# Two-block transformer kernel on one core: the RWKV triangular solve for both token tiles in common steps, gate scaling on GpSimd, constant tables in three transfers

## What is computed

```python
proj = (h @ w_in[l]).astype(jnp.float32)
ret_c, fox_c, rwkv_c, gate_c = jnp.split(proj, splits, axis=-1)
y_ret = _retention_branch(ret_c, ...)
y_fox = _fox_branch(fox_c, ...)
y_rwkv = _rwkv7_branch(rwkv_c, ...)
gates = jax.nn.sigmoid(gate_c)            # three gates of width 1024
merged = gates0 * (y_ret @ p_ret) + gates1 * (y_fox @ p_fox) + gates2 * (y_rwkv @ p_rwkv)
x = x + merged @ w_out[l]
x = x + (silu(g) * u) @ w_down[l]         # g, u = split(rmsnorm(x) @ w_gate_up[l])
```

## Time and profile before

| | us |
|---|---|
| median of 3 runs | 1142.59 (1142.31 to 1143.15) |
| the profiled execution | 1143.25 |
| its span | 1141.5 |
| PE busy | 1119.3 (98%) |
| DVE busy | 791.3 (69%) |
| ACT busy | 551.9 (48%) |
| POOL busy | 55.0 (5%) |
| chain that ended last, PE's share | 79% |

### The profile page before, as it was taken

The page is one execution under the profiler, slowest core; times in us unless marked ns, Lnnn a source line. Parts: engine busy times, 40 slices in busy tenths (PEclk is TensorE's granted clock), DMA queues, the critical chain, the costliest instruction groups (busy, mean ns, idle before and its releaser), DMA issues.

```text
span 1141.5 us, 22331 instructions
## 1 busy us (share of the span) xinstructions
PE 1119.3 (98%) x9556; PEld 1017.8 (89%) x9556; DVE 791.3 (69%) x1135; ACT 551.9 (48%) x768; POOL 55.0 (5%) x43
## 2 busy tenths in 40 slices
PE   9799999999999999999999999999999999999997
PEld 7689999899999998889998899999998778987687
DVE  6597765877555566887665966555567677877885
ACT  6355443534333344465443544333336675756762
POOL 0012000200000000102001000000000010001000
PEclk9899999999999999999999999999999999999998
DMA  9543334536453435542335356345344435363320
GB/s 365 212 173 113 112 113 153 205 125 240 202 219 137 196 140 217 175 158 98 126 113 205 128 207 236 144 189 220 147 148 171 167 114 197 133 227 111 113 110 38
DMA packets 27762, 188.28 MB, mean 165 GB/s; under 512 B 3488, under 2 KB 4384, under 8 KB 6048
## 3 DMA queue, kind: packets, MB, share of 16 engines
q1 hardware_dynamic: 26096, 175.89, 41.2%
q10 hardware_dynamic: 1440, 8.55, 1.9%
q0 software_dynamic: 144, 2.66, 0.5%
HBM read 181.84 MB, written 5.24 MB: 164 GB/s over the span
## 4 chain that ended last, share of the span: by engine, by line
PE 79%; DVE 9%; ACT 4%; DMA 2%; issue 1%; DVEq 1%; POOL 1%; POOLq 0%; ACTq 0%
PE bank L1149 21%; PE bank L696 14%; PE bank L1165 11%; PE bank L752 10%; PE bank L1129 4%; PE bank L1111 4%; DVE in_low L1971 2%; PE bank L1298 2%; PE bank L845 2%; ACT scratch L1526 2%; PE bank L861 1%; DMA table<-tables_dram 1%; PE bank L884 1%; ACT in_high L1459 1%; PE bank L684 1%
## 5 line engine op out<-in xcount | busy, mean ns | idle before, releaser
L696 PE MATMUL bank<-in_low,h_high 128*128 128x512 f32 x336 | 131.9, 393 | 0.0
L1149 PE MATMUL bank<-h_high,gate_split 128*128 128x256 f32 x704 | 128.8, 281 | 0.2
L1149 PE MATMUL bank<-h_high,up_split 128*128 128x256 f32 x704 | 128.6, 280 | 0.0
L1165 PE MATMUL bank<-act_split,down_split 128*128 128x256 f32 x960 | 118.5, 283 | 0.0
L696 PE MATMUL bank<-in_high,h_high 128*128 128x512 f32 x272 | 110.1, 405 | 6.7 <-DVE in_low L1971 6.0
L1165 PEld LDWEIGHTS bank<-act_split,down_split 128*128 128x128 f32 x960 | 116.6, 192 | 0.0
L752 PE MATMUL bank<-h_high,in_high 128*128 128x256 f32 x384 | 115.8, 301 | 0.5 <-DVE in_low L1971 0.5
L1149 PEld LDWEIGHTS bank<-h_high,gate_split 128*128 128x128 f32 x704 | 109.9, 189 | 0.8 <-DVE h_low L1913 0.6
L1459 ACT ACTIVATE in_high<-ring 128x2048 fp32r<-128x2048 f32 x46 | 87.7, 1910 | 47.0 <-PE bank L696 35.9
L1149 PEld LDWEIGHTS bank<-h_high,up_split 128*128 128x128 f32 x704 | 109.8, 189 | 0.0
L752 PE MATMUL bank<-x_low,in_high 128*128 128x256 f32 x384 | 108.4, 282 | 0.0
(11 more groups left out here) (380 smaller groups left out, 2509.3 us busy)
## 6 DMA issues: line engine op xcount, KB each, us to landing
ring<-w_in_dram SPq DMA_DIRECT2D x70, 1024.0 KB, 4.9
ring<-w_gate_up_dram SPq DMA_DIRECT2D x44, 1024.0 KB, 8.3
ring<-w_down_dram SPq DMA_DIRECT2D x22, 1024.0 KB, 4.9
ring<-w_out_dram SPq DMA_DIRECT2D x16, 1024.0 KB, 6.5
ring<-p_all_dram SPq DMA_DIRECT2D x6, 1024.0 KB, 4.8
x_kept<-scratch ACTq DMA_DIRECT2D x4, 1024.0 KB, 3.9
x<-x_kept ACTq DMA_DIRECT2D x4, 1024.0 KB, 7.6
table<-tables_dram POOLq DMA_DIRECT2D x1, 2594.0 KB, 13.7
```

The source lines that it names most:

```text
L696: last = mm(bank[(n - n % 2 + t) % 4][:], a, b, start=c == 0 and i == 0, stop=c == KT - 1 and i == 2)
L1149: last = mm(bank[2 * half + part][:, f * S:(f + 1) * S], a, b, start=k == 0 and i == 0, stop=k == KT - 1 and i == 2)
L1165: last = mm(bank[4 + m // 2][:, m % 2 * S:(m % 2 + 1) * S], a, b, start=first and m % 2 == 0 and k == 0 and i == 0, stop=end and m % 2 == ...
```

## The change

It does three things. (1) The solve runs both token tiles in the same steps: a level's product on PE holds both tiles, with two pieces of fill after it, and DVE's mask and addition are twice as wide. The buffers that both tiles shared are doubled. The order of all four engines in this stage is rewritten. (2) `gate_scale` goes from DVE to POOL, and POOL's `out_low` moves behind the second `variance_root`. (3) POOL's table transfer becomes three: `dshift` and `carry` (256 columns) before `norm(0)`, 1476 columns after it, and 3456 columns after the first root of layer 0. DVE's cast of `shift` moves behind `in_split` of group 5.

```diff
             def rt_matrices(l, t):
-                pe.wait_ge(*rt_T.after(l, 2 * t + 2))
                 if t == 0:
-                    pe.wait_ge(*y_T.after(l, 2))
+                    pe.wait_ge(*rt_T.after(l, 4))
                 else:
-                    pe.wait_ge(*rt_s.after(l, 2))
+                    pe.wait_ge(*rt_msk.after(l, 1))
+                    pe.wait_ge(*rt_at.after(l, 1))
...
-            def rt_level_p(l, t, v):
+            def rt_level_p(l, v):
...
-                    pe.wait_ge(*rt_qc.after(l, 5 * t + v - 1))
-                for i in range(2):
-                    if v < LEVELS - 1:
+                    pe.wait_ge(*rt_qc.after(l, v - 1))
+                for t in range(NT):
+                    for i in range(2):
+                        at = t * P + i * HD
+                        if v < LEVELS - 1:
...
             # PE's order
-                fill(l, 14, 16)
-                for t in range(NT):
-                    n = 16 + 17 * t
-                    rt_transposes(l, t)
-                    fill(l, n, n + 1)
-                    rt_matrices(l, t)
-                    fill(l, n + 1, n + 3)
-                    n += 3
-                    for v in range(1, LEVELS):
-                        rt_level_p(l, t, v)
-                        fill(l, n, n + 1)
-                        rt_level_q(l, t, v)
-                        n += 1
-                        if v < LEVELS - 1:
-                            fill(l, n, n + 1)
-                            n += 1
...
-                        fill(l, n, 48)
-                        rt_solve(l, 1)
-                        merge(l, 0, (0,))
-                        rt_chunk_terms(l, 1)
-                        merge(l, 0, (1,))
-                        rt_state(l, 2)
-                        merge(l, 0, (2,))
-                        rt_output(l, 1)
-                        merge(l, 0, (3,))
+                fill(l, 14, 15)
+                rt_transposes(l, 0)
+                rt_transposes(l, 1)
+                fill(l, 15, 17)
+                rt_matrices(l, 0)
+                fill(l, 17, 20)
+                rt_matrices(l, 1)
+                fill(l, 20, 23)
+                n = 23
+                for v in range(1, LEVELS):
+                    rt_level_p(l, v)
+                    fill(l, n, n + 2)
+                    rt_level_q(l, v)
+                    if v == LEVELS - 1:
+                        rt_ak_v(l)
+                    fill(l, n + 2, n + 4)
+                    n += 4
+                rt_solve(l)
+                fill(l, 43, 45)
+                rt_chunk_terms(l)
+                fill(l, 45, 47)
+                rt_output(l, 0)
+                rt_state(l, 1)
+                fill(l, 47, 48)
+                rt_state(l, 2)
+                merge(l, 0, (0,))
+                rt_output(l, 1)
+                merge(l, 0, range(1, 4))
                 merge(l, 1, range(3))
                 y_transposes(l, 2, w_y, y_ready, 2, y_tp, bank[4])
...
             # DVE
+                in_split(l, 4, in_hi, in_lo)
+                projected_low(0)
+                in_split(l, 5, in_hi, in_lo)
                 if l == 0:
-                    dve.wait_ge(consts_in.sem, 16)
+                    dve.wait_ge(shift_in.sem, 16)
                     for i, n in enumerate(("dshift", "carry")):
                         last = cp(shift[:, i], tab[n])
                     last.then_inc(shift_ok.sem, 1)
-                in_split(l, 4, in_hi, in_lo)
-                projected_low(0)
-                in_split(l, 5, in_hi, in_lo)
                 projected_low(1)
...
+                state_step(1)
+                variance(0)
+                state_step(2)
+                merged(0)
+                variance(1)
+                merged(1)
+                normed(0)
+                finished(0)
+                merged(2)
+                merged(3)
+                normed(1)
+                finished(1)
...
             # POOL
+            pool.wait_ge(ring_in[1].sem, 16)
+            pool.dma_start(table[:, N_FIRST:N_SHIFT], tables[:, N_FIRST:N_SHIFT]).then_inc(shift_in.sem, 16)
             pool.wait_ge(first_in.sem, 16)
             norm(0)
-            pool.wait_ge(ring_in[1].sem, 16)
-            pool.dma_start(table[:, N_FIRST:], tables[:, N_FIRST:]).then_inc(consts_in.sem, 16)
+            pool.dma_start(table[:, N_SHIFT:N_EARLY], tables[:, N_SHIFT:N_EARLY]).then_inc(consts_in.sem, 16)
...
+                gate_scale(0)
+                gate_scale(1)
+                variance_root(0)
+                gate_scale(2)
+                variance_root(1)
+                out_low(0, 0, 1)
+                out_low(0, 1, 2)
```

More of the change, by code:

```diff
@@ L127, in constant_tables @@
     t["near"] = qk((k % GRID_W >= cs) & (k % GRID_W < cs + NA_KW))
-    return {n: np.ascontiguousarray(np.broadcast_to(v, (P, v.shape[1])), dtype=np.float32) for n, v in t.items()}
+    late = ("rope_axial_c", "rope_axial_s", "rope_half_c", "rope_half_s", "window", "near")
+    order = [n for n in t if n not in late and n not in ("decay", "causal")] + ["decay", "causal", *late]
+    return {n: np.ascontiguousarray(np.broadcast_to(t[n], (P, t[n].shape[1])), dtype=np.float32) for n in order}
 BRANCHES = [1, 0, 2]
@@ L503, in build @@
         w_y, w_c2 = carve(11520, 512, 256)
+        w_state = carve(11264, 128)[0]
         w_f3 = st[:, 424:488]
@@ new lines, in rt_solve @@
+            def rt_solve(l):
+                pe.wait_ge(*rt_akc.after(l, 1))
+                pe.wait_ge(*rt_qc.after(l, LEVELS - 1))
+                for t in range(NT):
+                    for i in range(2):
+                        for c, o in corners:
+                            h = 2 * i + o
+                            last = mm(bank[4 + 2 * t + c][rows_of(c), h * P:(h + 1) * P].rearrange("p (a c) -> p a c", a=2),
+                                      m_tt[rows_of(c), c ^ o, 1, t, i], w_x[rows_of(c), t, :, h, :],
+                                      start=True, stop=True)
+                last.then_inc(rt_tx.sem, 1)
@@ L1675, in _ @@
-                    act.wait_ge(*rt_h.after(l, t + 1))
+                group(l, 14)
+                matrices_copied(0)
+                group(l, 15)
+                matrices_copied(1)
+                group(l, 16)
+                gate_tanh(l, 0)
+                for g in range(17, 20):
+                    group(l, g)
+                gate_tanh(l, 1)
+                group(l, 20)
+                act.wait_ge(*rt_ak.after(l, 1))
+                for t in range(NT):
+                    for c in range(2):
+                        last = f(w_x[rows_of(c), t, 1], bank[6 + c][rows_of(c), t * S:(t + 1) * S].rearrange("p (h v) -> p h v", h=NH), ACT.Copy)
@@ L1676, in _ @@
+                last.then_inc(rt_akc.sem, 1)
+                act.wait_ge(*rt_tx.after(l, 1))
+                for t in range(NT):
+                    for c in range(2):
+                        last = f(m_tz[t][rows_of(c)], bank[4 + 2 * t + c][rows_of(c), :].rearrange("p (h c) -> p h c", h=NH), ACT.Copy)
+                last.then_inc(rt_txc.sem, 1)
+                group(l, 21)
+                act.wait_ge(*rt_h.after(l, 1))
+                for t in range(NT):
                     for c in range(2):
-                        last = f(m_h[:, c], bank[4 + c][:, 0:P].rearrange("p (i v) -> p i v", i=2), ACT.Copy)
@@ L2265, in four @@
                     return ap.rearrange("p (h c) -> p h c", h=NH)
-                def gate_scale(l, i, half):
-                    dve.wait_ge(*g_out.after(l, 15 + 4 * i))
-                    g_ = gate[:, 16 - 8 * i + 4 * half:20 - 8 * i + 4 * half, :]
-                    last = tt(g_, g_, put(root[:], 1, 4), ALU.mult)
-                    if half:
-                        last.then_inc(gt_n.sem, 1)
                 lev = [tab["lev"][:, v * P:(v + 1) * P].rearrange("p (a c) -> p a c", a=2) for v in range(LEVELS)]
@@ L2352, in _ @@
-                    if t == 0:
-                        in_split(l, 19, in_hi, in_lo)
-                    else:
-                        merged(0)
-                    def state(n, source):
-                        for o in range(2):
-                            w = rows_of(o)
-                            last = tt(m_s[w, n, :, w], source[w], put(w_fe[w, n], 2, HD), ALU.mult)
-                        last.then_inc(rt_s.sem, 1)
-                    if t == 0:
-                        dve.wait_ge(*rt_hc.after(l, 1))
-                        dve.wait_ge(*rw_fe.after(l, 1))
-                        state(0, m_h[:, 0])
@@ new lines, in state, with state_step @@
+                def state(n, source):
+                    for o in range(2):
+                        w = rows_of(o)
+                        last = tt(m_s[w, n, :, w], source[w], put(w_fe[w, n], 2, HD), ALU.mult)
+                    last.then_inc(rt_s.sem, 1)
+                def state_step(n):
+                    dve.wait_ge(*rt_sm.after(l, n))
+                    a = w_state.rearrange("p (i v) -> p i v", i=2)
```

(4 more changed lines are left out.)

334 lines of the change are left out of this document (146 added, 188 removed).

## The result

| | before | changed kernel |
|---|---|---|
| median | 1142.56 us (4 runs, 1142.31 to 1143.15) | 1133.22 us (4 runs, 1132.78 to 1133.94) |
| profiled execution, its span | 1143.25, 1141.5 | 1133.94, 1132.1 |
| ratio of the times | | 0.9916, 95% interval 0.990 to 0.9932 |

The changed kernel is 9.3 us faster. The prediction was 1135.8, range 1127.0 to 1139.2: right in sign and in range, 2.6 us too high.

What follows compares the result with a forecast made beforehand. PE, busy 98% of the span, was taken as the bound. Start -7.0 and per layer -4.9 + 0.7 + 0.1 + 4.2 = +0.1, for two +0.2, gave 1135.8 us, range 1127.0 to 1139.2.

Steps and rivals of the forecast that it cites:

- The start: Before `rw_difference`: splitting the table transfer and moving the cast removes PE's gap before group 4 and low clock; 7.0 us gained, once.
- rival (c): At the start, group 5's load still lands at 37 and PE waits 4.1 at `rw_difference`: gain 3.5, 1139.3 us; chance 0.06.
- The wait of 0.6 before `rw_difference`: At the start, PE wants `rw_difference` at 38.8 but DVE finishes `rw_low` at 39.4, so PE waits 0.6 us.
- group 4's load: At the start, the 128 KB shift table shares queues with first loads: group 4 at most 0.3 us late, costing nothing, at worst 0.3.
- Joined steps: In the solve, twelve pairs of steps join per layer, each saving 0.34 us, and small waits go: 4.9 us gained per layer.
- new waits: In the solve, group 16's half splits end 0.2 late and PE's second output waits 0.5: 0.7 us lost per layer.
- The levels keep up: In the solve, the chain between levels takes 7.7 to 7.9 of 8.3 us, slack 0.4 to 0.6, so levels cost nothing.
- Rival (b): In the solve, the level chain is late by 0.4 us in each of four levels, twice: 1139.0 us; chance 0.10.
- The end of the solve: POOL's `gate_scale(2)` and `out_low` hold DVE operations, so merge block 6 and the transposes of y wait: 4.2 us lost per layer.
- the two operations of `finished(0)` each wait for half of `out_low`: At the solve's end, both DVE operations are held by POOL until 13.4 us after the second output, delaying merge block 6.
- Rival (a): In the solve, the port shared by DVE and POOL costs little, without the 4.2 and 0.1 losses: 1127.2 us; chance 0.22.
- rival (d): In the solve, long PE waits lower its clock and two successive POOL operations keep the port: 1147.0 us, slower; chance 0.04.

Runs made afterwards that it cites:

- The version in which little else costs: The changed kernel with gate operations back on DVE, ACT's tanh of gates 0 and 1 moved later, and `out_low` in eight POOL pieces: 1127.42 us, ratio 0.987.
- gates on DVE: The changed kernel with its six gate operations per layer put back on DVE, ACT's order left alone and `out_low` still on POOL: 1139.99 us, ratio 0.9962.
- `out_low` twice: The changed kernel with the suspected cost doubled: POOL adds zeros to each half of `out_low` after computing it: 1146.50 us, ratio 1.0027.
- all on DVE: The changed kernel with the gate operations back on DVE and `out_low` there too, as one operation behind `merged(4)`: 1133.72 us, ratio 0.9911.
- cast moved: The kernel before with only DVE's cast of `shift` moved behind the split of group 5, table still in one transfer: 1139.75 us, ratio 0.9967.

## Why the prediction was right, and where its sizes were off

**The start (7.0 predicted; 6.4 in the profiled run, 6.3 to 7.2 over all ten with three transfers): right.** Cast behind the splits, clock at 1.00, group 5's load no longer the brake: each as the working had it, and the experiment with the cast alone gave the half that rival (c) had priced (3.5; measured 3.4). Two details were wrong. The wait of 0.6 before `rw_difference` did not show, because group 4 was already late by more than that. And "nothing, at worst 0.3" for group 4's load: it landed 0.9 later. The traces don't blame the shift table for more than that 0.3: ACT began group 4 at 29.17, 28.46 and 30.12 in the three kernels with one transfer, and at 29.14 to 30.14 in the ten with the shift table ahead. The two means are 0.3 apart, which is too little to tell from the spread. The load's landing varies by up to 1.7 us, for a cause that these traces don't show, and the sum should have carried that as a range.

**Joined steps (4.9 per layer gained, less 0.7 of new waits): right.** Steps stand 4.16 apart against 4.14. The version in which little else costs gained 3.8 and 4.4 per layer, against 4.2. Fill 20 starts 0.2 late (0.41 after the matrices) and the second output 0.3 (the idle time printed at 192.63), where the working had 0.2 and 0.5.

**The levels keep up: right.** Rival (b) is out: no level step of the change waited for DVE. DVE's 512-wide pair takes 1.28 (1.3 taken). `gate_scale(1)` met the half splits as foreseen (1.71 and 2.22 instead of 1.22), and PE did not feel it. But the slack was as thin as said: with the gates on DVE one half split started 2.4 us late (149.44; in the change 147.68, less the 0.7 by which that run was ahead), and PE waited 2.1.

**The end of the solve (4.2 lost per layer; measured 2.8): the mis-sized term.** The working ran on time for 8 us. With the second output at 192.63 as zero, `variance(1)`'s input came at 2.9 (3.0 predicted), it was held until 5.2 (5.2) and ended at 6.8 (6.8), and `out_low` began at 8.55 (8.3). The step that failed is "the two operations of `finished(0)` each wait for half of `out_low`". Root and hand-over took 0.25 longer, and so the first of them (L2319, at 200.92) slipped in before POOL began at 201.18. The second was held for the first half; then came `merged(2)` and `merged(3)`, with an input in PSUM, and ran beside POOL's second half for 1.3 us, so that only 0.96 was left to hold `normed(1)`. `finished(1)` ended at 15.2, not at 16.6. Of two full holds, 4.7 us, 2.95 came true. The forecast of this order was a matter of luck, and one kernel shows both outcomes. In gates on DVE the same race (here `finished(0)` is L2326 and L2329) went as in the change in layer 0, where L2326 started 0.26 before POOL's `out_low`; in layer 1 it started 0.09 behind it, and both operations were held as predicted:

```profile
623.48 2.55 DVE L2326 TENSOR_TENSOR scratch<-scratch 128x256 f32<-128x256 f32 x1 [0.43 <-issue]
626.10 2.41 DVE L2329 TENSOR_TENSOR scratch<-scratch 128x256 f32<-128x256 f32 x1
...
623.39 4.84 POOL L2696 TENSOR_TENSOR out_low<-ring,out_high 128x1024 fp32r<-128x1024 f32 x2
```

`finished(1)` then ended 15.0 us behind the second output instead of 13.5. So about 1.4 us a layer in a chain of six operations hung on a quarter of a us, and the range should carry that. Rival (a), the port costing little, is refuted: taking the holds away by other means was worth up to 3 us a layer.

**The balance.** Predicted -7.0 and +0.2; measured -6.4 and -2.7, with -0.2 in the rest. The prediction had the whole gain of the joined solve (4.2 net) given back at its end; two thirds of it were (2.8). The smaller gain at the start hid a part of this, so the total came out closer than the solve's term.

**The port.** The rows and the dose test show that a DVE operation with both inputs in SBUF, or the small one-input L2019, waits for the end of a large POOL operation, and that reductions (L2017, 0.42 at 195.51 beside `gate_scale(2)`) and operations on PSUM do not. The rule of the Trainium skill on which the prediction leaned ("SBUF — State Buffer", section "SBUF: two separate sides": the shared pair is locked for a whole instruction) agrees with the two-input operations that were held and with those on PSUM and the reductions that were not. The same rule also names DVE operations in a mode that uses two ports; whether L2019, which has one input, ran in such a mode no run here shows. By that rule the other engine is blocked until the instruction ends; who is let in between two instructions in a row it doesn't say. Here it was the one that waited.

**The slower rival (d): its mechanism exists, its condition wasn't met.** It wanted PE pauses in the solve long enough to lower the clock and two POOL operations in a row that keep the port. The longest pause in the change was 1.8 us from start to start (1.6 more than the usual step) and the clock stayed at 1.00. With `out_low` twice the pause was 5.7 us, the clock fell, and the kernel came out slower than before, by 3.3 us.

## What to carry over

An engine's share of busy time doesn't say where it has slack: DVE was busy 69% of the span and had not one free us in the 20 before the projection, so work given to GpSimd "for free" came back as holds at just that place. When an engine is in such a stretch, keep GpSimd's two-input operations out of it, or cut them into short pieces; moving them within it changed nothing here. And when an operation changes its engine or its place, look at who waits for it in order: what is queued behind that wait (here ACT's rounding behind a tanh) can cost more than the operation.

## What was not expected of the hardware

**The port changes hands between two instructions.** A DVE operation that waits gets in before POOL's next one starts: two POOL operations in a row took 5.72 instead of 4.68 us around DVE's half split, and eight pieces of `out_low` 6.46 around five DVE operations. The first, in the change:

```profile
154.59 5.72 POOL L2692 TENSOR_TENSOR arena<-arena,root 128x1024 f32<-128x1024 f32 x2 [29.09 <-ACT arena L1516]
156.34 1.71 DVE L1983 TENSOR_TENSOR in_low<-ring,in_high 128x1024 fp32r<-128x1024 f32 x1 [2.77 <-ACT in_high L1476]
```

**The same pause may or may not cost the clock.** In the two versions with the late tanh, the same pause, 2.28 us from start to start on PE, stood in both layers. Windows of 5 us behind it, of gates on DVE (layer 0, layer 1) and then of all on DVE (layer 0, layer 1):

```profile
155.00:160.00 5.00, 5.00 (x97) 4.80 (x96) 2.83 (x4) 2.14 (x2) 0.00 (x0) 1.00 0.58 210
575.00:580.00 5.00, 5.00 (x88) 4.80 (x87) 1.16 (x2) 2.40 (x2) 0.00 (x0) 0.74 0.42 138
```

```profile
155.00:160.00 5.00, 5.00 (x91) 4.80 (x91) 1.06 (x1) 2.40 (x2) 0.00 (x0) 0.85 0.49 167
575.00:580.00 5.00, 5.00 (x96) 4.80 (x96) 2.26 (x3) 2.40 (x2) 0.00 (x0) 1.00 0.47 162
```

In one layer of each the clock stayed at 2.4 GHz, in the other it fell for a part of the window; the 24 fill matmuls there took 4.36 us (first to last start) instead of 2.86. It is likely why gates on DVE spread over 7 us from run to run: its six runs of 1140.0 us and more have a mean granted clock of 0.992 or 0.993, its five of 1138.3 and less 0.995 or 0.996. Only one of them was profiled by stage. Counted from start to start as well, pauses of 4.2 us (cast moved), 5.7 us (`out_low` twice) and 6.2 us (before) lowered the clock each time they were seen. Those of up to 1.9 us never did, nor did the one of 2.1 us before a merge block in layer 1 of gates on DVE.
